# Low halves of the weights from latent attention to the end of sparse attention: accumulating DMA in place of GpSimd's subtractions

## What is computed

```
x = first_block(x)                    # mixers (pool, linear, forgetting attention) and a gated FFN
h = rmsnorm(x) ; z = h @ w_in_2       # split into q_lat, c_kv, k_rope, z_a, q_b, k_b, v_b, z_b, q_idx, ...
q = rmsnorm(q_lat) @ w_uq ; kv = rmsnorm(c_kv) @ w_ukv
y_a = softmax(q k_a^T * scale + chunk mask) @ v_a * silu(z_a)          # latent attention, 8 heads
score = sum_h relu(q_idx k_idx^T) * w_idx ; keep = top_k(score, 128)   # indexer
y_b = softmax(q_b k_b^T + rel. bias, kept keys only) @ v_b * silu(z_b) # sparse attention, 8 heads
x = x + (sigmoid(gate_a) * (y_a @ w_o_a) + sigmoid(gate_b) * (y_b @ w_o_b)) @ w_out
out = rmsnorm(x)
```

## Time and profile before

| | |
|---|---|
| median of three runs | 1031.28 us |
| the profiled execution | 1031.6 us, of which the span of the instructions is 1029.7 us |
| TensorE busy over the span | 1014.3 us |
| VectorE / ScalarE / GpSimd busy | 670.4 / 510.2 / 339.0 us |
| GpSimd's subtractions (L2717) | 256 in the program, 203.2 us |
| stretch of the change | 597 to 912 us of the span |

### The profile page before, as it was taken

How to read it: one execution, slowest core, us unless ns; L and a number is a source line. 1 busy time by engine, 2 the same in 40 slices (tenths; PEclk the granted TensorE clock), 3 DMA queues, 4 the chain that set the end, 5 groups by cost and what they waited for, 6 DMA issues and landing times.

```text
span 1029.7 us, 15320 instructions
## 1 busy us (share of the span) xinstructions
PE 1014.3 (99%) x5694; PEld 847.6 (82%) x5694; DVE 670.4 (65%) x1256; ACT 510.2 (50%) x936; POOL 339.0 (33%) x404
## 2 busy tenths in 40 slices
PE   9999999999999999999999999999999999999996
PEld 7887877788889999999997778767987777788885
DVE  6875657566657667777767657899756765235553
ACT  6432656547734444444445547446755555223333
POOL 1354532442221111111104657333436766421101
PEclk9999999999999999999999999999999999999998
DMA  8322233227945455454435736211223332322312
GB/s 291 105 66 84 83 85 103 63 62 193 217 111 126 100 133 123 97 139 123 104 92 143 177 110 201 62 62 62 82 83 102 91 115 85 100 90 94 102 62 81
DMA packets 43688, 113.49 MB, mean 110 GB/s; under 512 B 5584, under 2 KB 9104, under 8 KB 43616
## 3 DMA queue, kind: packets, MB, share of 16 engines
q1 hardware_dynamic: 36720, 96.80, 29.4%
q0 software_dynamic: 6480, 15.21, 9.1%
q10 hardware_dynamic: 416, 0.52, 0.2%
HBM read 104.41 MB, written 4.74 MB: 106 GB/s over the span
## 4 chain that ended last, share of the span: by engine, by line
PE 80%; DVE 9%; ACT 4%; issue 2%; POOL 2%; SPq 1%; DMA 1%; DVEq 0%; ACTq 0%; POOLq 0%
PE bank L1777 17%; PE bank L1778 16%; PE bank L1779 16%; PE bank L1793 5%; PE bank L1792 5%; PE bank L1791 5%; PE bank L1941 2%; PE bank L1932 2%; POOL acc L2753 1%; DVE score L2622 1%; PE bank L1825 1%; PE bank L1827 1%; PE bank L1826 1%; DVE m L2620 1%; PE bank L1917 1%
## 5 line engine op out<-in xcount | busy, mean ns | idle before, releaser
L2717 POOL TENSOR_TENSOR WL<-WS,WH 128x256 fp32r<-128x256 f32 x256 | 203.2, 794 | 250.6 <-ACT WH L1995 234.7
L1777 PE MATMUL bank<-HH,WH 128*128 128x512 f32 x600 | 243.6, 406 | 0.7 <-ACT f_v L2030 0.3
L1779 PE MATMUL bank<-HH,WL 128*128 128x512 f32 x600 | 234.6, 391 | 0.0
L1778 PE MATMUL bank<-HL,WH 128*128 128x512 f32 x600 | 234.3, 390 | 0.0
L1995 ACT ACTIVATE WH<-WS 128x1024 fp32r<-128x1024 f32 (+1 forms) x130 | 133.5, 1034 | 5.5 <-DMA WS<-wall 3.5
L1777 PEld LDWEIGHTS bank<-HH,WH 128*128 128x128 f32 x600 | 113.2, 189 | 27.9 <-issue 3.8
L1779 PEld LDWEIGHTS bank<-HH,WL 128*128 128x128 f32 x600 | 112.6, 188 | 24.6
L1778 PEld LDWEIGHTS bank<-HL,WH 128*128 128x128 f32 x600 | 113.1, 188 | 20.8 <-issue 1.2
L2484 DVE TENSOR_TENSOR WL<-SS,WH 128x512 fp32r<-128x512 f32 x112 | 76.0, 692 | 43.6 <-ACT WH L2139 43.3
L2139 ACT ACTIVATE WH<-SS 128x512 fp32r<-128x512 f32 x112 | 66.9, 624 | 74.6 <-DVE SS L2481 57.4
L2759 POOL DMA_DIRECT2D SS<-wall x32 | 27.6, 862 | 213.0 <-DVE SS L2481 141.9
(11 more groups left out here) (374 smaller groups left out, 2279.0 us busy)
## 6 DMA issues: line engine op xcount, KB each, us to landing
WS<-wall SPq DMA_DIRECT2D x129, 512.0 KB, 3.5
SS<-wall SPq DMA_DIRECT2D x48, 256.0 KB, 3.6
SS<-wall POOLq DMA_DIRECT2D x32, 256.0 KB, 4.1
WL<-wall POOLq DMA_DIRECT2D x13, 512.0 KB, 7.8
scratch<-rows SPq DMA_DIRECT2D x8, 320.0 KB, 5.0
b_t<-scratch SPq DMA_DIRECT2D x8, 256.0 KB, 3.4
X<-xT SPq DMA_DIRECT2D x7, 256.0 KB, 6.1
outT<-X SPq DMA_DIRECT2D x7, 256.0 KB, 2.5
```

The source lines that it names most:

```text
L1777: e.matmul(b[:, :], wh, xh, start=k == 0, stop=False)
L1778: e.matmul(b[:, :], wh, xl, start=False, stop=False)
L1779: m = e.matmul(b[:, :], wl, xh, start=False, stop=k == n - 1)
L2717: e.tensor_tensor(WLS[:, at_c:at_c + 256], WS[:, u % NST, cs], f32(WHS[:, at_c:at_c + 256]), ALU.subtract).then_inc(*tick(w_low_g, u if c ...
```

## The change

One line: from the latent projections to the end of sparse attention the low halves come by `"dma"`. `now["look"]` stays 2, and so does all else.

```diff
-        now["low"] = w_low_g
+        now["low"] = "dma"
         side = chain(latents(), mla_v(), mla_products(0))
```

## The result

The changed kernel took 1044.82 us (median of 4 runs, 1044.42 to 1045.77), the kernel before 1031.42 us in the same comparison (1031.19 to 1031.68): a ratio of 1.0131, 95% interval 1.0119 to 1.0144. It is 13.4 us slower, where 3.7 us were forecast. The sign was right; the time lies well above the range.

A forecast was written before the change was run, and what follows sets the result against it. TensorE's matmuls were taken to set the pace (busy 311.4 of 315 us). Late low halves 2.1 + 0.5 and ScalarE 0.8 + 0.3 gave 3.7 us, 1035.0 us on the median; forecast's own range 1032.8 to 1037, 8-in-10 range 1030.6 to 1039.5.

The forecast's parts named there:

- the near zero for the removed subtractions: GpSimd's 168 subtractions, some 125 us, lie under TensorE's work; removing them is worth 0 on the path by itself.
- the term for late low halves: Main term: low halves coming by DMA land after TensorE wants them, at two units, 2.1 + 0.5 us.
- The unit at 721.72: Tightest unit, 6.3 us from rounding to first matmul; its low half was to come 2.1 us late.
- the one at 900.98: First of two units rounded back to back, 9.4 us to its matmul; late by 0 to 0.9, taken as 0.5 us.
- What is added on ScalarE: 42 negated copies of 1.06 us, most fitting into ScalarE's waits in attention; two places were to cost 0.8 and 0.3 us.
- The place at 803: TensorE's wait for `PT` at 802.67: negation adds 1.06 us, less 0.26 for VectorE's relief, so 0.8 us.
- That at 829: TensorE's product with `PT` at 829.43: 0.73 us of slack against a negation of 1.06, so 0.3 us.
- the four places that I named as signs of being wrong: Near 689, 716, 859 or 882, more than 1 us from `PT` copies counted as covered would show the forecast wrong.
- The relief of VectorE: Without subtractions VectorE's scaling (L2450) runs less slowed by GpSimd; credited 0.26 us in the chain at 803.
- That GpSimd would be held up at the issue: Rival: from 770 on VectorE's L2450 delays each DMA issue by 0.36 to 0.95 us; sum 4.2 us, 1035.5; chance 0.05.
- have about as much or more: All units besides the three tightest were said to have about 9.8 us or more, up to 24, before their first matmul.
- the crowded rival: Low-half DMAs land as slowly as at 236 to 290 (median 7.9 us): sum 6.5 us, 1037.8; chance 0.13.

The follow-up runs named there:

- e3: The kernel before with one small DMA (128 x 64 B, memory to memory) issued by GpSimd ahead of each of the 42 units' subtractions: 1035.09 us, ratio 1.0034.
- e8: The changed kernel without ScalarE's 42 negated copies, each DMA waiting for the rounding alone, output not the reference's: 1035.27 us, ratio 1.0034.
- e1: The kernel before with ScalarE's 42 negated copies added, GpSimd's subtractions waiting for them and overwriting them: 1039.39 us, ratio 1.0076.
- e6: The changed kernel with a tiny GpSimd memset right behind each accumulating DMA's issue: 1045.27 us, ratio 1.0133.
- e7: The changed kernel with SyncE's copies of rows to scratch moved behind the second product block of latent attention: 1045.00 us, ratio 1.0128.
- e4: The changed kernel until the values of sparse attention, GpSimd's subtractions again behind them, 21 of 42 units by DMA: 1038.09 us, ratio 1.0063.
- e2: The changed kernel with units rounded three units ahead in place of two (two around the values of both attentions): 1050.59 us, ratio 1.0185.
- e11: The changed kernel with the 42 negations on GpSimd, ahead of its DMA issues, in place of ScalarE: 1057.40 us, ratio 1.0249.

## Why the prediction was wrong

Right were the sign, what bounds the kernel, the near zero for the removed subtractions (e3 and e8 gain 0.3 us at 803, e3 with the subtractions still there), and the term for late low halves where I looked. The unit at 721.72 was to cost 2.1 us and cost 2.6 (its landing took 6.42 us and not 6.0); the one at 900.98 was to cost 0.5 and cost 0.7; the median landing was to be near 6 us and was 6.1.

**The step that failed is "What is added on ScalarE": 1.1 us, measured 6.0.** "Most copies fit into such a wait. They cost where TensorE stands ready at the product of `PT` with the values": I looked for places with a unit just ahead and no slack, found two, and took every other place as covered. The place at 803 was found and given 0.8 us; it cost 1.4 in the changed kernel and in e1. That at 829 was given 0.3 and cost 2.1. Others I had as covered: 1.0 us at 793 to 800, 0.3 at 822 to 826, 1.2 at 851 to 859. Of the four places that I named as signs of being wrong (689, 716, 859, 882) only the third lost anything, 0.2 us. The flaw is that I compared one copy with one slack. The way to `PT` goes from ScalarE to VectorE and back to ScalarE, for one pair of heads after the other, and a unit's copy stands in it at every second or third step; a copy covered in one step has used the slack of the next. That is how I read the rows; no run moved a single copy to test it. e8 shows the size: with all DMAs in place and no copies, nothing is lost there.

**The relief of VectorE, a credit in two terms, turned round.** "L2450 has a maximum near 0.5 us": the median did fall, but eight VectorE instructions are held for 1.1 to 1.7 us, where in before no L2450 took over 1.07 us in all. What each part does, shown by taking it away: hold without copies costs nothing (e8), copies with a short hold cost 3.1 us (e6; with the subtractions in the place of the DMAs, e1, 5.2), both cost 6.0 us. So the 6.0 us are neither's alone. The likely reading is that the copies use up the slack, and the hold of 1.5 us then lies open. That GpSimd would be held up at the issue, a rival of mine, shows in no row: all 42 issues took 0.86 to 1.03 us. It was VectorE that waited. The Trainium skill (SBUF — State Buffer, "Who interferes with whom") says that whichever comes first keeps the shared ports for its whole instruction and the other is blocked. The trace agrees in so far as GpSimd's issue came first, and shows the hold lasting past the issue, through the next GpSimd instruction.

**A late low half that I had with those that "have about as much or more".** The unit rounded at 618.76 has 10.1 us to its matmul (630.24 - 1.42 - 618.76) and needs 2.44 + 8.90 = 11.3; it costs 1.7 with what follows. I used 6.0 us for the landing everywhere, by which it had 1.6 to spare. In the rows of before it had 11.2 us (628.75 - 617.54), so the landing alone would have made it late by 0.1; the rest is the rounding's own wait of 1.20 us for its load. "No unit waits for its load before, so that is worth 0 too" held for the kernel before and not for the changed one. From 612 to 640 the DMA share was 0.66 before and is 0.98 now; that the load is late for this, too, is likely and not shown. The landing lies beside SyncE's copies of rows to scratch, and without these it took 7.42 (e7), against 8.90 and 9.61 with them (the changed kernel and e4). I had judged the crowd by the DMA share at 720, not at 620; the crowded rival was right at this place.

**The end was not in the sum.** 42 DMAs more on GpSimd make its closing drain longer than the landing of the outputs that covered it, 1.9 us. No row of before would have given a price, but the row of the drain was there to be asked about. e3 shows it apart from all else.

In sum: forecast 2.6 + 1.1 + 0 = 3.7, measured 4.9 (landings) + 6.0 (sparse attention) + 1.9 (drain) = 12.8 us of span. Without the 42 negated copies 9.4 us of it go (e8); part of the same microseconds goes without the hold (e6). What the DMAs cost without them is some 3 us.

No version tried beats the kernel before. e8's remainder shows why none of this kind is near: even with the negation for nothing, the landings and the drain cost some 3 us. The waits of the earlier trace rows got much shorter nowhere but in e2 and e11, where TensorE comes far later; e3 and e8 lost the 0.2 us at 803.

## What to carry to other kernels

An operation added to an engine with 50% load need not be covered by its idle time when that idle time is the other side of a ping-pong with a second engine. Follow the whole chain to what the bounding engine waits for, over several rounds, and subtract every added piece from the same slack. Before accepting a rework that frees an engine nobody waits for, price what it puts on engines that are waited for: here 125 us of GpSimd were worth next to nothing, and without 1.06 us on ScalarE, 42 times, 9.4 us of the loss were gone. Ask of every transfer that grows what else uses the DMA engines at that very place: the plain loads came late, too. And look at the end of the program: something that was hidden behind the outputs may no longer be.

## What the runs showed of the hardware

- GpSimd's closing drain took 4.5 us with 45 DMAs issued by GpSimd in the program, 4.7 with 66, 6.4 with 87 (8 KB or 512 KB each alike) and 8.4 with 129. Up to 66 it may be covered by the landing of the outputs.
- A VectorE scaling, or an addition of two SBUF operands, that starts in a GpSimd DMA issue of 0.88 us with a mask addition right behind was held until that had run (0.29 to 1.84 us), in eight cases. With a memset of one column in between, the excess stays under 0.9 us.
- TensorE's granted clock fell behind some waits and not behind others. In e6 TensorE waited 3.5 us, and in e7 2.3 and 1.9 us, in these windows (columns as in the earlier trace rows), in which a part runs at the lower level of 1.2 GHz:

```profile
628.00:642.00 14.00, 10.49 (x45) 8.50 (x44) 8.19 (x15) 8.24 (x15) 4.50 (x6) 0.88 1.05 293
```

```profile
728.00:742.00 14.00, 11.67 (x80) 10.46 (x78) 9.24 (x29) 11.03 (x23) 1.72 (x2) 0.88 1.02 248
836.00:846.00 10.00, 8.08 (x36) 5.02 (x35) 4.38 (x11) 4.28 (x9) 3.84 (x5) 0.83 0.53 100
```

The changed kernel's profile had the waits of 2.3 and 1.9 us at the same two places with a clock of 1.00, and e4's had waits of 2.8 and 2.4 us with 1.00. In e7 this cost some 3 us, and its runs spread over 4 us where the kernel before spreads over 1.2. The Trainium skill (TensorE: Matmul & The Clock Gate, Part 1) says that the chip judges activity on a beat of its own, which does not start with the kernel. By that the same wait could cost clock in one execution and not in another. The rows fit that; no run was made to show it.
